# One block of a hybrid transformer on one core: the 512-token halves of each GEMM tile move outside the contraction loop

## What is computed

```python
# first block
proj = rms_norm(x, g) @ w_in                     # 1024 -> 2560 columns (20 weight tiles of 128)
mix  = concat([attention, rwkv7], -1) @ w_out    # 8 tiles
x    = x + rms_norm(mix, g)
u    = rms_norm(x, g) @ w_up                     # 64 tiles
u    = conv_b + sum(conv_w[j] * shift(u, j) for j in range(3))
gate, val = split(u, 2)
f    = (gelu(gate) * val) @ w_down               # 32 tile products, 4 groups of 8
x    = x + rms_norm(f, g)
# second block
h = rms_norm(x) * (1 + scale) + shift            # scale, shift, gate from c @ w_ada + b_ada
p = h @ w_in_2                                   # 29 tiles
y = concat([gla, hgrn, stick_breaking], -1) @ w_out_2   # 8 tiles
out = rms_norm(x + gate * y) * final_w
```

## Time and profile before

| | |
|---|---|
| median of 3 runs | 3233.01 us (3232.54 to 3235.76) |
| the profiled execution, its own time | 3237.68 us |
| its span in the profile | 3235.9 us |
| mean granted TensorE clock | 0.874 of 2.4 GHz |
| PE busy with matmuls | 2706.5 us, 84% |
| matmuls of L370 (all GEMM tiles) | 7728 |
| chain that ended last, share of L370 | 53% |

### The profile page before, as it was taken

How to read it: one execution, slowest core, us unless ns; L and a number is a source line. 1 busy time by engine, 2 the same in 40 slices (tenths; PEclk the granted TensorE clock), 3 DMA queues, 4 the chain that set the end, 5 groups by cost and what they waited for, 6 DMA issues and landing times.

```text
span 3235.9 us, 45658 instructions
## 1 busy us (share of the span) xinstructions
PE 2706.5 (84%) x17970; PEld 2133.0 (66%) x17970; DVE 1213.7 (38%) x1572; ACT 726.4 (22%) x1050; POOL 796.0 (25%) x448
## 2 busy tenths in 40 slices
PE   2899565677689599999999999993999948879986
PEld 1787334666667278888888888871888836653374
DVE  2634536444442653123213213317000056544343
ACT  2111551121121222012102101203111253225521
POOL 1344000000003133433434343340343333210011
PEclk7999657898889799999999999997999955559988
DMA  5411000000002111111111111121211100000031
GB/s 165 156 40 54 5 1 31 3 3 3 3 28 91 65 39 52 45 51 46 46 51 45 52 45 52 45 72 84 91 52 46 46 20 1 0 3 1 0 124 58
DMA packets 34892, 146.85 MB, mean 45 GB/s; under 512 B 3656, under 2 KB 5832, under 8 KB 33608
## 3 DMA queue, kind: packets, MB, share of 16 engines
q1 hardware_dynamic: 23184, 84.42, 7.9%
q10 hardware_dynamic: 11576, 60.50, 5.1%
HBM read 124.46 MB, written 20.45 MB: 45 GB/s over the span
## 4 chain that ended last, share of the span: by engine, by line
PE 72%; DVE 16%; ACT 6%; issue 3%; DMA 2%; DVEq 1%; ACTq 1%; POOL 0%; POOLq 0%
PE ps L370 53%; PE ps L734 2%; DVE xx L76 2%; ACT ab L76 1%; DVE s_m L76 1%; PE ps L787 1%; PE ps L564 1%; DVE proj L76 1%; DVE x_lo L76 1%; DVE lvl L76 1%; DVE ps L76 1%; DMA bias_table<-bias_row 1%; DVE zz L76 1%; PE ps L554 1%; PE ps L561 1%
## 5 line engine op out<-in xcount | busy, mean ns | idle before, releaser
L302 POOL TENSOR_TENSOR w_hi<-w_raw,small 128x1024 fp32r<-128x1024 f32 x161 | 306.5, 1904 | 2200.2 <-PE ps L370 2193.4
L370 PE MATMUL ps<-x_hi,w_hi 128*128 128x512 f32 x2064 | 644.0, 393 | 92.3 <-DVE x_lo L76 85.8
L370 PE MATMUL ps<-x_lo,w_hi 128*128 128x512 f32 x2064 | 639.5, 391 | 0.0
L370 PE MATMUL ps<-x_hi,w_lo 128*128 128x512 f32 x2064 | 639.0, 391 | 0.0
L370 PEld LDWEIGHTS ps<-x_hi,w_hi 128*128 128x128 f32 x2064 | 387.3, 189 | 184.8 <-issue 71.4
L370 PEld LDWEIGHTS ps<-x_lo,w_hi 128*128 128x128 f32 x2064 | 390.2, 189 | 81.7
L370 PEld LDWEIGHTS ps<-x_hi,w_lo 128*128 128x128 f32 x2064 | 389.8, 189 | 81.8
L305 POOL TENSOR_TENSOR w_lo<-w_raw,w_hi 128x1024 fp32r<-128x1024 f32 x161 | 405.8, 2521 | 12.6
L76 DVE SCALAR_TENSOR_TENSOR cv<-ps,cst,cv 128x1023 f32<-128x1023 f32 x64 | 82.1, 1283 | 258.1 <-ACT cv L76 252.7
L370 PE MATMUL ps<-f_hi,w_lo 128*128 128x512 f32 x512 | 157.6, 389 | 0.0
L370 PE MATMUL ps<-f_lo,w_hi 128*128 128x512 f32 x512 | 157.6, 389 | 0.0
(11 more groups left out here) (255 smaller groups left out, 3404.9 us busy)
## 6 DMA issues: line engine op xcount, KB each, us to landing
w_raw<-wall SPq DMA_DIRECT2D x161, 512.0 KB, 3.4
ada_w<-wada ACTq DMA_DIRECT2D x24, 512.0 KB, 5.3
x_spill<-x ACTq DMA_DIRECT2D x2, 4096.0 KB, 11.0
x<-x_spill ACTq DMA_DIRECT2D x2, 4096.0 KB, 13.3
x_in<-xT ACTq DMA_DIRECT2D x2, 2048.0 KB, 12.1
x<-xT ACTq DMA_DIRECT2D x1, 4096.0 KB, 13.5
gate_spill<-gate_st ACTq DMA_DIRECT2D x8, 512.0 KB, 2.6
gate_in<-gate_spill ACTq DMA_DIRECT2D x8, 512.0 KB, 3.3
```

The source lines that it names most:

```text
L302: nc.gpsimd.tensor_tensor(w_hi[:, u, :, :], w_raw[:, u, :, :], sm["one"].unsqueeze(2).to_broadcast([P, KT, P]), ALU.mult).then_inc(S("w_hi ...
L370: last = mm(ps[:, 2 * u + h, :], w[:, u, k, :], x[:, k, h * 512:(h + 1) * 512], start=(k == 0 and w is w_hi and x is hi), stop=(k == KT - ...
```

## The change

In `gemm`, the loop over the two halves `h` of the tokens goes from the innermost place to the outermost. Before, each weight piece was used for the first and then for the second 512 tokens, so the output bank alternated with each matmul. After, 24 matmuls go to the bank of the first 512 tokens, over the whole contraction, and then 24 to the other bank. The waits for `parts` are made in the first pass only. The number of matmuls, their operands, the waits ahead of the tile and the signal at its end are the same.

```diff
-                for k in range(KT):
-                    if parts is not None:
-                        pe.wait_ge(S(parts[0]), parts[1] + (k + 1))
-                    for w, x in ((w_hi, hi), (w_hi, lo), (w_lo, hi)):
-                        for h in range(2):
+                for h in range(2):
+                    for k in range(KT):
+                        if h == 0 and parts is not None:
+                            pe.wait_ge(S(parts[0]), parts[1] + (k + 1))
+                        for w, x in ((w_hi, hi), (w_hi, lo), (w_lo, hi)):
                             last = mm(ps[:, 2 * u + h, :], w[:, u, k, :], x[:, k, h * 512:(h + 1) * 512],
                                       start=(k == 0 and w is w_hi and x is hi),
                                       stop=(k == KT - 1 and w is w_lo))
```

## The result

The changed kernel takes 3276.73 us (median of 4 runs, 3272.8 to 3285.27), the kernel before 3234.39 on the same chip (4 runs, 3232.54 to 3236.76): ratio 1.0134, interval 1.0112 to 1.0156, some 42 us more. The profiled execution of the kernel after took 3285.27 us, the longest of its four, with a span of 3283.5 us against 3235.9.

A forecast was written before the change was run, and what follows sets the result against it. PE's pace and its waits were taken as the bound. 13.7 + 1.7 + 16.0 - 1.6 + 4.8 + 4.0 = 38.6 us on the median 3233.01 gave 3271.6 us, range 3260 to 3284.

The forecast's parts named there:

- Steady tiles: 152 of 161 tiles wait for nothing new; their pace stays the same, 0 us.
- faster and slower: Bank change each matmul costs 13.4 ns: 3168 us (5%); adding to one bank is slower: up to +1240 us (3%).
- Tiles 28, 124, 153: Tiles fed by `x_lo`: 27 matmuls left after the last low part, +4.56 us each, plus 1.6 each for slow clock.
- Tile 20: Tile fed by `x_lo` that began with most of its steps ready: +1.7 us.
- Four waits for `f_lo`: First down tile of each FFN group: PE reaches step 7 after 21 matmuls and waits, 4 x 4.0 = 16.0 us.
- Their clock: Slow clock after the four `f_lo` waits: between 0 and 2.2 us each, taken as 1.0, 4.0 together.
- Tiles 0 to 2: Kernel start: tile 2 begins without the idle 5.03 us and with the clock up, -1.6 us, between -2.6 and 0.
- the clock holds: Rival: after the new waits the clock stays up, so the waits alone cost +28.8 us, 3261.8 us; 20%.
- Every wait cools: Rival: PE drops to slow clock after every wait, +48.0 us, 3281.0 us; 20%.
- My half-and-half case: Main forecast: the waits with part of the clock's cost, +38.6 us, 3271.6 us; 50%.
- One sign I gave: In tiles fed by `x_lo`, PE's waits should grow by about 0.7 us a step, with three matmuls fewer between them.

The follow-up runs named there:

- the filled kernel: New order only in the down tiles fed by `f_lo`, 14 unused matmuls ahead of each of four waits, against the kernel before: 3251.8 us, ratio 1.0034.
- the mirror image: New order only in the 52 tiles called with `parts`, old order in the other 109, against the kernel before: 3281.27 us, ratio 1.0119.
- step 7 after 27: In down tiles fed by `f_lo`, the first half's step 7 comes after 27 matmuls, old order elsewhere, against the kernel before: 3251.76 us, ratio 1.0032.
- the first paired kernel: First two tiles of three x-fed products run step by step together, second one or two steps behind, against the kernel before: 3232.79 us, ratio 0.9967.

## Why the prediction was right, and where its sizes were off

The forecast was 3271.6 us in 3260 to 3284, 38.6 us more than before. Measured are 3276.73 us, some 42 us more by the medians. By its own working the range should have ended at 3233.0 + 48.0 + 1.6 = 3282.6 us, not at 3284; the measured time lies inside either. The terms one by one, from the profiled executions:

- **Steady tiles, 0 us: confirmed.** 663 matmuls in 150 us both before and after, and 1036.64 us for the chain's piece with half the tiles in the new order. The rivals that rested on the bank, faster and slower, have both fallen.
- **Tiles 28, 124, 153, 4.56 each and 1.6 of clock: the waits right, the clock too small.** From the end of the last `x_lo` to the next tile it is 7.78, 8.45 and 8.56 us, 1.61 before in each: 6.17, 6.84 and 6.95 us more, 20.0 in all for my 18.5. Less 4.56 each, the clock has taken 1.6, 2.3 and 2.4 us. That is half of the time at 0.50 behind the last `x_lo`, 3.2, 4.7 and 4.8 us. The step that was off is the 2.2 us "less 3 x 0.2 = 0.6 that pass in step 6": it took the slow clock as starting with step 6, as long as behind the idle 5.03 us, while PE had been at 0.50 for all of the feeding in tiles 28 and 124 and from its middle on in tile 153. In the two other runs with the new order in these tiles the same places give 1.0 to 2.3 us, so the 1.6 for tile 28 is a hit by luck.
- **Tile 20, 1.7:** 1.9 us.
- **Four waits for `f_lo`, 4.0 each: right.** 4.05 each by the filled kernel. The distance of 7.39 us, DVE's 1.23 us and 21 matmuls gave it.
- **Their clock, 1.0 each between 0 and 2.2: too small.** 1.6 each, 6.3 in all for my 4.0. The step that was off is "between 0 and 2.2, I take 1.0", taken because the waits were shorter than 5.03 us. All four cooled PE, and so did all twelve in the three other runs with this order in these tiles; the clock fell between 1.6 us before PE started again and 1.5 us after. The Trainium skill (TensorE: Matmul & The Clock Gate, section HAM oscillation — how this bites in real kernels) describes a loop in which each wait for data leaves the matmuls behind it at half clock. The kernel after agrees with it, 0.50 behind each of the four, though the first matmuls behind the first wait still went at full pace. The waits of 2.4 us, shorter than those of its example, kept 1.00 in two of four cases.
- **Tiles 0 to 2, -1.6:** -0.9 us. The idle 5.03 us of the earlier trace rows have gone, as forecast: 270 matmuls are one piece of the chain. But it takes 64.17 us for 270 x 0.2267 = 61.2, so 3.0 us of slow clock. Of these, 2.2 lie behind the last `x_lo`, for my 1.6.

Sum: 20.0 + 1.9 + 16.2 + 6.1 - 0.9 = 43.3 us, where 892.5 us for the stretch of the kernel after gives the 6.1. This is 4.7 over the forecast, and nearly all of it is the clock's: 1.5 us in the three tiles, 2.1 behind the waits for `f_lo`, and 0.7 by which tiles 0 to 2 fell short. The profiled spans differ by 47.6 us, 4.3 more. Those lie outside the edited places: 6.2 us more in the stick-breaking attention, 164.0 us at clock 0.91 before and 170.2 us at 0.87 after, and 1.9 us less elsewhere. The change isn't needed for it: the run with the old order in the fed tiles has 170.2 us there as well, and the mirror image 161.8. The profiled execution is also 8.5 us above its own median.

Of the rivals, "the clock holds" is excluded by the stretches at 0.50. "Every wait cools" had the behaviour right and the price too high: it had 16.6 us for the clock in these places, and they measure 6.3 + 6.1 = 12.4, so the time fell between it and the forecast. My half-and-half case had the better number by a price that erred one way and a count that erred the other.

One sign I gave came in one place only. The waits for `x_lo` in a fed tile were to grow by 0.7 us a step, since three matmuls fewer lie between them. At tile 153, where the three matmuls still went at full pace, a wait grew from 2.42 to 3.11 us. Ahead of step 6 of tile 28 the wait was 1.04 us and is 1.05 now: three matmuls at 0.43 us last as long as six at 0.227. The slow clock hid there in a row that did not change, and only the granted clock showed it (0.50 in 1126 to 1142, against 0.85 before).

## What to carry to other kernels

Where a consumer follows a producer step by step, count the work that is left when the last piece comes, and the work that lies ahead of it: in this kernel that, and not the total, is what the order of the loops decided. The order that uses a step up entirely was the better one, and taking a second tile into the same steps is better still (16.5 us here), if what then comes early (here a clear on DVE, a weight split on POOL) is moved out of the way. Each new wait in a dense piece is to be priced with the slow clock behind it, here 1.6 us on 3.9.

## What the runs showed that I had not expected

- At tile 124, fed a step each 3.5 us, the clock rose to 1.00 and held it with six matmuls a step; with three it was 0.50 to the end of the feeding, in the kernel after and in both runs with the new order there. The old order is not safe either: at tile 153 the clock fell to 0.50 under it in two runs (old order in all fed tiles, step 7 after 27), and tile 154 began 1.2 to 1.3 us later than in the kernel before.
- Idle 2.4 us between dense stretches cooled PE in two of four cases of one execution, at the same place of the same loop; idle 3.75 us in 16 of 16, over four executions; and the two waits of 1.8 and 1.9 us in the first paired kernel both cooled it.
- Matmuls of no use to the result, put into a wait, keep the clock at 1.00 and were worth 6.3 us over four waits, though the kernel does more work.
- Adding 24 times running to one bank and changing the bank with each matmul go at one pace, 226.7 ns.
